# A two-layer block in one kernel: the input projections in another order, with the delta gate last

## What is computed

```python
h = rmsnorm(x, norm_w)
aq, ak, av, az, dq, dk, dv, dz, b_f, a_f, b_b, a_b = split_proj(h @ w_in)
# eight heads of 64: q and k normalised, each token attends to a patch of 8 x 16 in a 16 x 64 grid
attn = neighbourhood_attention(aq, ak, av, rpb) * silu(az)
# four heads of 128: centred depthwise convolution of width 5, silu, l2 norm of q and k
dq, dk, dv = split(silu(conv(concat(dq, dk, dv), conv_w)))
# chunks of 64; per chunk a triangular system is solved, then a scan over the chunks, forwards and backwards
o = gated_delta(dq, dk, dv, g_f, beta_f) + flip(gated_delta(flipped, g_b, beta_b))
delta = rmsnorm(o) * dn_norm_w * silu(dz)
x = x + concat(attn, delta) @ w_out
```

## Time and profile before

| | us |
|---|---|
| median of 3 runs | 2304.66 |
| lowest and highest run | 2299.58 and 2307.76 |
| span of the profiled execution | 2301.0 |
| TensorE busy in the span | 2206.9 |
| VectorE busy | 1093.5 |
| ScalarE busy | 936.8 |
| GpSimd busy | 380.9 |

### The profile page before, as it was taken

One profiled execution on the slowest core, in us unless ns is written; L12 is line 12 of the kernel. 1 busy time (PEld: TensorE's weight loads), 2 busy tenths in 40 slices (PEclk: granted clock), 3 DMA queues, 4 the chain that ended last, 5 costly groups with the idle time before them and its releaser, 6 DMA issues.

```text
span 2301.0 us, 29061 instructions
## 1 busy us (share of the span) xinstructions
PE 2206.9 (96%) x11559; PEld 1800.5 (78%) x11559; DVE 1093.5 (48%) x2025; ACT 936.8 (41%) x1705; POOL 380.9 (17%) x596
## 2 busy tenths in 40 slices
PE   8999999898997899999999999999999999999998
PEld 6778777676796688788887788887888888888886
DVE  5454545443256343566555664655514243433441
ACT  4544544343364143456455554543313233232220
POOL 5200112644403110000000000003301111010111
PEclk9999999999598899999999999999999999999999
DMA  4621345353743231111110211112221111344232
GB/s 142 221 82 58 86 127 171 109 149 101 242 157 92 110 124 52 42 49 62 34 59 23 65 56 46 37 46 69 64 66 55 37 56 55 119 140 158 93 105 87
DMA packets 171384, 209.76 MB, mean 91 GB/s; under 512 B 36576, under 2 KB 124752, under 8 KB 169712
## 3 DMA queue, kind: packets, MB, share of 16 engines
q1 hardware_dynamic: 150752, 141.51, 19.6%
q0 software_dynamic: 20496, 66.39, 9.0%
HBM read 150.41 MB, written 53.77 MB: 89 GB/s over the span
## 4 chain that ended last, share of the span: by engine, by line
PE 86%; DVE 5%; ACT 4%; issue 1%; DMA 1%; POOL 1%; SPq 0%; DVEq 0%; POOLq 0%; ACTq 0%
PE PS L1730 12%; PE PS L1732 12%; PE PS L1731 12%; PE PS L1724 9%; PE PS L1726 9%; PE PS L1725 9%; PE PS L1690 5%; PE PS L2018 3%; PE PS L1997 3%; PE PS L1801 2%; PE PS L1827 2%; DVE WH L2439 2%; PE PS L2050 1%; PE PS L2063 1%; DMA RAW<-in_w_in 1%
## 5 line engine op out<-in xcount | busy, mean ns | idle before, releaser
L1730 PE MATMUL PS<-WH,HH 128*128 128x512 f32 x1344 | 546.8, 407 | 19.3 <-DVE WH L2439 10.7
L1732 PE MATMUL PS<-WH,HL 128*128 128x512 f32 x1344 | 528.1, 393 | 0.0
L1731 PE MATMUL PS<-WH,HH 128*128 128x512 f32 x1344 | 527.2, 392 | 0.0
L1724 PE MATMUL PS<-HH,WH 128*128 128x512 f32 (+1 forms) x976 | 399.5, 409 | 4.2 <-DVE WH L2439 4.2
L1726 PE MATMUL PS<-HH,WH 128*128 128x512 f32 (+1 forms) x976 | 382.9, 392 | 0.0
L1725 PE MATMUL PS<-HL,WH 128*128 128x512 f32 (+1 forms) x976 | 382.3, 392 | 0.0
L1730 PEld LDWEIGHTS PS<-WH,HH 128*128 128x128 f32 x1344 | 254.8, 190 | 78.8 <-DVE WH L2439 11.8
L1732 PEld LDWEIGHTS PS<-WH,HL 128*128 128x128 f32 x1344 | 254.0, 189 | 55.2
L2439 DVE SCALAR_TENSOR_TENSOR WH<-RAW,WK,WH 128x512 fp32r<-128x512 f32 (+2 forms) x248 | 188.0, 781 | 221.4 <-ACT WH L2072 220.8
L1731 PEld LDWEIGHTS PS<-WH,HH 128*128 128x128 f32 x1344 | 255.3, 190 | 46.2
L1724 PEld LDWEIGHTS PS<-HH,WH 128*128 128x128 f32 (+1 forms) x976 | 183.0, 187 | 43.7 <-DVE WH L2439 5.7
(11 more groups left out here) (313 smaller groups left out, 2923.2 us busy)
## 6 DMA issues: line engine op xcount, KB each, us to landing
RAW<-in_w_in SPq DMA_DIRECT2D x200, 256.0 KB, 2.9
RAW<-in_w_out SPq DMA_DIRECT2D x32, 256.0 KB, 3.5
sig_d<-WK POOLq DMA_DIRECT2D x32, 256.0 KB, 2.3
WK<-sig_d POOLq DMA_DIRECT2D x32, 256.0 KB, 3.2
WK<-in_rpb POOLq DMA_DIRECT2D x16, 480.0 KB, 5.6
RAW<-in_w_in SPq DMA_DIRECT2D x32, 192.0 KB, 2.6
dnc_d<-TM SPq DMA_DIRECT2D x12, 512.0 KB, 3.6
TM<-dnc_d SPq DMA_DIRECT2D x10, 512.0 KB, 4.6
```

The source lines that it names most:

```text
L1724: e.matmul(ps, wh, hh, start=k == 0, stop=False)
L1730: e.matmul(ps, hh, wt[:, 0:width], start=k == 0, stop=False)
L1731: e.matmul(ps, hh, wt[:, 512:512 + width], start=False, stop=False)
L1732: mm = e.matmul(ps, hl, wt[:, 0:width], start=False, stop=k == 7)
```

## The change

`X` is put in another order: the four `dn` blocks, the four `na` blocks, then `dz`. So `dn0` is now the block of the start, its six tiles of q, k and v at once, and its evacuation and convolutions begin when the norms of the tokens are there. `dz` is planned once `da` of the second pair of heads is (`plan.drain(has("da", 1))`). Its tiles are copied by ScalarE into `TM[:, 2]`. That space is free when the images and the score matrices are stored (waits on `c_im` and `c_pa`). Silu, the multiply with the norm weights and the store are done on halves of four tiles (`zs`). The gather of the last pair's values, made by 24 DMAs of SP and 8 of GpSimd in two parts, is made by GpSimd as for the other pairs. The loads of heads 2 and 3, and `fz`, wait for `zs`.

```diff
@@ -140,7 +140,7 @@
 
 
 NSLOT, XSLOT, NRAW = 11, 10, 4
-X = ["dz", "dn0", "dn1", "dn2", "na0", "dn3", "na1", "na2", "na3"]
+X = ["dn0", "dn1", "dn2", "dn3", "na0", "na1", "na2", "na3", "dz"]
 SB = ["h0", "h1", "h2", "m00", "h3", "h4", "h5", "m01", "h6", "h7"]
 RT = ["q0", "v0", "q1", "m10", "v1", "q2", "v2", "q3", "v3", "m11"]
 FIN = ["sb0", "sb1", "rt0", "rt1", "o0", "o1"]
...
@@ -417,10 +417,14 @@
     slots = {}
     uses = Counter()
 
+    def waiting(held):
+
+        return held and held[:2] == ("tile", 0) and ("g", *held[1:], 7) in plan.known and ("ev", *held[1:]) not in plan.known
+
     def take(item):
         ring = state["ring"]
         state["n"] += 1
-        if ring[state["n"] % len(ring)] == state["open"]:
+        while ring[state["n"] % len(ring)] == state["open"] or waiting(holder.get(ring[state["n"] % len(ring)])):
             state["n"] += 1
         bank = ring[state["n"] % len(ring)]
         place[item] = (bank, holder.get(bank))
...
@@ -492,24 +496,26 @@
         plan.spawn(first_out(b))
 
     def first_out(b):
-        for t in range(8):
-            yield has("xs")
-            yield has("g", b, t, 7)
-            slot(("ev", b, t), "stg", 3)
-            put("ev", b, t)
-            plan.now[0] += 1200.0
-            if t in (1, 3):
+        yield has("xs")
+        for th in range(2):
+            put("xb", th)
+            yield
+        put("dg")
+        for c in range(3):
+            if c == 2:
+                yield has("co", 0, 0)
+            for th in range(2):
+                yield has("g", b, (c, th), 7)
+                put("ev", b, (c, th))
                 yield
-                put("xb", t // 2)
-            yield
-        put("dg")
+            plan.spawn(conv(0, c))
 
     def gemm(b, ready=None, after=None):
         tiles = tiles_of(b)
-        if BLOCKS[b] == "dz":
+        if b == 0:
             together(b, tiles[:6])
         n_slot = XSLOT if b < 9 else NSLOT
-        for t in tiles[6:] if BLOCKS[b] == "dz" else tiles:
+        for t in tiles[6:] if b == 0 else tiles:
             if ready:
                 ready(t)
             end = t == tiles[-1]
...
@@ -575,15 +582,13 @@
             yield has("no", p - 1, 1, 7)
         else:
             yield has("ge")
-        for part in range(2) if p == 3 else (0,):
-            yield has("ev", BLOCK[f"na{p}"], 5 if p == 3 and part == 0 else 7)
-            for g in range(4):
-                put("nv", p, g, part)
-                yield
-        if p < 3:
-            put("nz", p)
-            yield
-            put("nx", p)
+        yield has("ev", BLOCK[f"na{p}"], 7)
+        for g in range(4):
+            put("nv", p, g)
+            yield
+        put("nz", p)
+        yield
+        put("nx", p)
 
     def table():
         n = tabs[0]
...
@@ -611,14 +616,8 @@
                 else:
                     turn(kind, p, h, i)
                 yield
-        if p == 3:
-            yield has("d9", 1, 14)
         if ("no", p, 1 - h, 7) in plan.known and ("nw", p) not in plan.known:
             put("nw", p)
-            if p == 3:
-                put("nz", p)
-                yield
-                put("nx", p)
 
     tabs = [0]
 
...
@@ -726,6 +725,12 @@
             plan.spawn(na_front(p, h))
             plan.spawn(na_back(p, h))
 
+    def gate_side():
+        for half in range(2):
+            yield has("ev", BLOCK["dz"], 4 * half + 3)
+            put("zs", half)
+            yield
+
     plan.spawn(solve())
     for name in X:
         b = BLOCK[name]
...
@@ -733,8 +738,9 @@
             plan.drain(has("nw", int(name[2]) - 2))
         if name[:2] == "na":
             plan.spawn(na_side(int(name[2])))
-        if name == "na3":
-            rows(3)
+        if name == "dz":
+            plan.drain(has("da", 1))
+            plan.spawn(gate_side())
         gemm(b)
         if name == "dn0":
             plan.spawn(gates())
...
@@ -744,19 +750,15 @@
                 use_ring([0, 1], "na")
                 for _ in range(NTAB):
                     table()
-            if n < 3:
-                rows(n)
+            rows(n)
 
 
 
     def share():
 
         yield has("g", X_LAST, 7, 7)
-        yield has("nv", 3, 3, 1)
-        yield has("da", 0)
         plan.both(*((kind, h) for h in range(2) for kind in ("dl", "dv")), ("dt", 0), ("dt", 1))
-        yield has("nw", 2)
-        yield has("da", 1)
+        yield has("zs", 1)
         plan.both(("dl", 2), ("dv", 2), ("dt", 2))
         yield has("nw", 3)
         plan.both(("dl", 3), ("dv", 3), ("dt", 3))
...
@@ -1542,13 +1545,6 @@
                     for n in range(72, 76):
                         load(n)
 
-                elif kind == "nv" and a[0] == 3 and not (a[2] and a[1] < 2):
-                    p, g, part = a
-                    w.wait_ge(*at["ev", BLOCK["na3"], 7 if part else 5, "out"])
-                    for h in range(2):
-                        w.wait_ge(*at["no", p - 1, h, 7, "m"])
-                    gather(lambda o, i, sem: e.dma_start(o, i).then_inc(sem, 16), p, g, c_v3[part][g],
-                           slice(3, 4) if part else slice(0, 3))
                 elif kind == "nx":
                     p = a[0]
                     w.wait_ge(*at["nz", p, "z"])
...
@@ -1636,6 +1632,7 @@
                     w.wait_ge(c_im, 224 * (n + 1))
                     if h == 2:
                         w.wait_ge(c_pa, 128)
+                        w.wait_ge(c_zst, 32)
                     if h == 3:
                         for done in na_read():
                             w.wait_ge(*done)
...
@@ -2134,12 +2129,10 @@
                         continue
                     w.wait_ge(*at["g", b, t, 7, "done"])
                     if name == "dz":
-                        i, n = slots[item]
-                        w.wait_ge(c_stg[i], 16 * n)
                         w.wait_ge(*at["xs", "r"])
-                        e.activation(stg[i], ps, ACT.Silu, scale=rs[:, 72 + t:73 + t]).then_inc(*w.sig(*item, "z"))
-                        if t == 7:
-                            e.preload_act_table_set(LN_EXP)
+                        w.wait_ge(c_im, 448)
+                        w.wait_ge(c_pa, 128)
+                        copy(gate_tile(t), ps, rs[:, 72 + t:73 + t]).then_inc(*w.sig(*item, "out"))
                     else:
                         if name in ("na2", "na3"):
                             w.wait_ge(c_mix[buf_of(b)], 256)
...
@@ -2164,6 +2157,12 @@
                             o = tokens(buf_of(b))[:, t, :]
                         copy(o, ps, rs[:, 72 + t:73 + t] if name[:2] == "na" else None).then_inc(*w.sig(*item, "out"))
 
+                elif kind == "zs":
+                    half = a[0]
+                    z = gate_half(half)
+                    w.wait_ge(*at["ev", BLOCK["dz"], 4 * half + 3, "out"])
+                    e.activation(z, z, ACT.Silu).then_inc(*w.sig(*item, "z"))
+                    e.preload_act_table_set(LN_EXP)
                 elif kind == "nq":
                     p, u = a
                     w.wait_ge(*at[(*item, "v")])
...
@@ -2862,18 +2859,16 @@
                         before = n - NTAB
                         w.wait_ge(*at["ns", before // 4, before % 2, before // 2 % 2 * 4 + 3, "s"])
                     dma(tab[n % NTAB], rpb[n // 4 * 2 + n % 2, n // 2 % 2], c_tab[n % NTAB])
-                elif kind == "ev":
-                    b, t = a
-                    name = BLOCKS[b]
-                    if item in slots:
-                        i, n = slots[item]
-                        w.wait_ge(*at[(*item, "z")])
-                        w.wait_ge(c_dn, 80)
-                        z = stg[i].rearrange("p (h c) -> p h c", h=4)
-                        e.tensor_tensor(z, z, dnw.unsqueeze(1).to_broadcast([128, 4, 128]),
-                                        ALU.mult).then_inc(*w.sig(*item, "out"))
-                        w.wait_ge(*w.last)
-                        dma(dz_d[t * 128:(t + 1) * 128, :], stg[i], c_stg[i])
+                elif kind == "zs":
+                    half = a[0]
+                    z = gate_half(half).rearrange("p (h c) -> p h c", c=128)
+                    w.wait_ge(*at[(*item, "z")])
+                    w.wait_ge(c_dn, 80)
+                    e.tensor_tensor(z, z, dnw.unsqueeze(1).to_broadcast([128, 16, 128]),
+                                    ALU.mult).then_inc(*w.sig(*item, "m"))
+                    w.wait_ge(*w.last)
+                    dma(dz_d[half * 512:(half + 1) * 512, :].rearrange("(t p) c -> p t c", p=128),
+                        gate_half(half).rearrange("p (t c) -> p t c", t=4), c_zst)
                 elif kind == "ed":
                     b, t = a
                     name = BLOCKS[b]
```

More of the change, by code:

```diff
@@ L316, in work @@
     if kind == "nv":
-        return [("pool", 2330)] if a[0] < 3 or a[2] and a[1] < 2 else [("dma", 3500)]
+        return [("pool", 2330)]
     if kind == "d9":
@@ L531, in gemm @@
```

(8 more changed lines are left out.)

43 lines of the change are left out of this document (18 added, 25 removed).

## The result

The changed kernel takes 2339.61 us, median of four runs (2335.25 to 2343.13), against 2304.48 us for the kernel before, also four runs (2299.58 to 2307.76). The ratio is 1.0168, with a 95% interval of 1.0138 to 1.0198: slower, by about 35 us. The forecast was 2309, no change, with a range up to 2321. The prediction was wrong.

A forecast was written before the change was run, and what follows sets the result against it. TensorE, busy 96% of the span, was taken to bound the kernel, with only the 764.35 us before `wo0` movable. Scans 9.3 us late less 5 returned gave +4.3 us, span 2305.3, median 2309; range 2295 to 2321.

The forecast's parts named there:

- the convolutions behind `dn0`: a new wait: Delta blocks after the new start: TensorE waits for convolutions, 11 us and then 8 us, 19 us in all.
- The clock: Rival: the clock falls in the new waits behind `dn0`, two `dn1` tiles give 9 us more; time 2318, chance 0.24.
- The first wait: In `dn1`, before the norms of head 0: TensorE waits 11 us for convolution work on VectorE and ScalarE.
- The second: Behind head 0's first norms: the third part's chain, with only two raw buffers, makes TensorE wait 8 us.
- 20 us for attention under `dz`: Last pair's attention, moved beside `dz` at the full clock, puts the last projection's end 20 us later.
- 20 - 1: Up to the last projection's end: 20 us more for the moved attention, less 1 us gained at the start.
- The sign of being wrong: `dz` ending before 590 or after 606 us; the forecast had it near 598 us.
- The bare load: After `dz`: no matmul until head 0 lands, 14.6 us plus 0.3 us; levels begin at 613.0 us.
- The levels: After head 0's load: 19.1 us at the low clock, 5.1 us idle dropped; scans begin at 632.1 us.
- From the first scan to `wo0`: Scans begin 9.3 us late at 632.1 us and win back 5 us; `wo0` near 769 us.
- The table loads in the first wait: Before head 0's norms: three ScalarE table loads at 1.28 us; at the skill's 2.66 us the forecast would be 2311.8.
- The images rival: Rival: ScalarE's copy of the first `dz` tile waits for image stores; late by 8 us gives 2317, chance 0.09.

The follow-up runs named there:

- the fillers alone: 12 filler matmuls of 512 columns in TensorE's wait before head 0's norms, in the changed kernel with the zero fill held back: 2316.74 us, ratio 1.0065.
- both edits: Changed kernel with the zero fill held back until `dn1`'s first tile ends and `dn1` to `dn3` evacuations planned apart: 2313.51 us, ratio 1.0055.
- The first edit: Changed kernel with the zero fill put after `dn1` in the planned order; it was still issued at 53 us: 2335.33 us, ratio 1.0140.
- the variant with 25 fillers: Kernel with both edits plus 15 filler matmuls before head 0's load and 10 before its images: 2322.49 us, ratio 1.0083.

## Why the prediction was wrong

**What failed is the term of 19 us for "the convolutions behind `dn0`: a new wait".** It stood for all that the new start costs up to T. What T lost came to 57 us, 31.3 idle and 25.8 by the clock, and some 48 us of it lie in the delta blocks. Three things were left out of the term.

- *A step that moves along.* The DMAs of `zs` and of the loads were followed to their new places, and those of `dg` were not. The zero fill was never named. Where it stood before, TensorE was busy for all of 75 to 100 us, and no load of weights went out behind it till 104.0 us. Held back: 12 us less.
- *The clock.* It was a rival, at 9 us, with 0.24, and the sum took nothing. Its mechanism was right, in its place too: the fillers alone gave 11 us, 6 of them seen in the delta blocks. The point from which it decides, that the slow tiles aren't hidden in the next wait, was answered by that run: they aren't. A wait of over ten us before dense work should have had its price in the sum, not in a rival, since the earlier trace rows had shown it.
- *The halts.* The sum took the 11 us before head 0's norms as the price of the chain of VectorE and ScalarE. It is the price of the planner's order: with the evacuations apart that wait is gone, `dn1` takes 46.0 instead of 67.5 us, and `dn1` to `dn3` run at 0.97. Behind `dn1` the sum had nothing. There the idle time is indeed no longer than before, 3.9 us in `dn2` and `dn3` against 4.0 in `dn1` and `dn2`, but the clock is 0.90 instead of 0.98; with the evacuations apart it is 1.00 and these two blocks take 7.5 us less than with the held fill alone. In the time it is worth 9 to 14 us, which overlaps with the clock's 11, so the three don't add up to 35 us one by one.

Point by point, the rest:

- The first wait, "TensorE waits 11 us": 12.2 us with the fill held back. The chain was rightly read for that order: from the first Silu at 79.19 us to the norms at 86.41 it took 7.2 us there, where the sum had 7.0. The second, 8 us, came as several short ones, 6.8 us together in that variant, of which some stood before too. The idle sum of 19 is near there, and only there.
- 20 us for attention under `dz`: near. What T has gained in work is 16.4 us by the estimate above, where the forecast had 20 - 1, and `dz` runs at 0.98. Its cover is thin, though. When the projections get ahead of the inversions, as with both edits, the attention is bare again.
- The sign of being wrong, `dz` ending after 606 us, came true at 633.5.
- The bare load, 15.0 us to the first level: 14.2. The levels, 19.1 us, at the low clock: 19.4. From the first scan to `wo0` the forecast had 136.9 us, by its own times; the trace has 134.8. Behind T the forecast had 171.0 us and the trace has 168.4. The Trainium skill's clock rule (TensorE: Matmul & The Clock Gate, section What's actually happening), that only activity lifts the clock, agrees with the fillers, which took the norms from 6.96 to 3.73 us.
- The table loads in the first wait, priced at 1.28 us by the row. It is so again in the changed kernel, with the next work right behind:

```profile
83.59 1.28 ACT L2217 ACT_TABLE_LOAD   x1
84.89 0.22 ACT L2217 ACTIVATE WK<-PS 128x64 f32<-128x64 f32 x1
```

The Trainium skill (ScalarE: Activation LUTs, section What ACT_TABLE_LOAD costs) gives 2.66 us for the switch, of which 1.28 are the load itself, as in the row, and the rest a drain. No trace here shows the drain: these rows follow each other without a gap.

- The images rival: `dz` began 0.6 us behind `na3`, and the last inversion step ended 2.1 us into it. It cost nothing to speak of in the changed kernel.
- The median stood 1.7 us under the profiled span this time, where I had put it 3.7 above. That is scatter: the profiled run was the slowest of the four.

**What stays open.** With both edits the kernel is still some 13 us behind the one before; its T, 600.4 us, is nearly the forecast's 598, but by another way, with `dz` 34 us late. What a `dz` not tied to the inversions would give was not tried, since its tiles lie where the inversions work. The first edit's order was not run with the held fill alone, so its own share in the later variants is not known. Held fill, evacuations apart and fillers before the norms were not run together. Single traces of the same plan differ by up to 6 us in T: with both edits the pairs took 326.5 us in one and 332.0 in another, with 26.3 and 35.7 us busy at the low clock. Gains below that are read from the medians.

## What to carry to other kernels

Moving a block to the front moves everything that hung on its end. List each queue's next item at the new place, the transfers without a reader among them, and ask what load goes out right behind. Price a new wait before dense matmuls, here one of 12.2 us, with the clock it drops, in the sum. And where a planner halts the main engine for a buffer, plan the evacuation apart from the next tile: here that was worth 9 to 14 us in the new order and 7 in the old. And if you move an item in a planner's order, hold the order of every engine against the one before, since the planner may have moved others too.

## What was not expected of the hardware

- Bulk transfers of GpSimd's queue hold small loads of SP's queue for about as long as they take themselves: behind 5.8 MB of zeros, whose large parts took 10.7 us to land, 192 KB took 13.7 us instead of 2.9. Small stores behind it on GpSimd's own queue fared the same: 256 KB took 10.9 us instead of 2.5.
- The filler of 512 f32 columns shows as two matmul records and took 0.87 us (30 records in 13.04 us for 15), where transposes of 128 columns had suggested 0.43.
- TensorE was busy and at the low clock all the same. In 640 to 660 us, in the variant with 25 fillers, it was busy 19.6 of 20 us with the small matmuls of levels and scans, at a clock of 0.50. In the variant with both edits and no fillers it was busy 31.15 of 34.1 us in 508.9 to 543 us, with attention, at 0.56, and its `dn1` to `dn3` and `dz`, full of 512-column projections, ran at 0.97. Small matmuls aren't always slow: in the kernel before the scans up to 700 us ran at 1.00, 63.04 of 65.7 us busy. What decides is not shown.
- Idle TensorE time filled with matmuls that nobody reads paid 11 us in one place and nothing that the times can tell in another.
